# FFN up as seven products of half-size blocks, its convolution summed in PSUM, and FFN down with its first two tiles together in the second half too

## The reference

```
x = x + g1 * out_x                        # end of the mixer
hx = modulate(rms_norm(x, norm2_g), sh2, sc2)
gate, val = split(hx @ ffn_w_up, 2)       # ffn_w_up: 1024 x (2 * 2816)
gate = dwconv_grid(gate, w, b, 16, 64)    # 3x3 taps per channel on a 16 x 64 grid of tokens
x = x + g2 * ((silu(gate) * val) @ ffn_w_down)
return rms_norm(x, final_g)               # goes into the attention layer
```

## Time and profile before

| | us |
|---|---|
| median of 3 runs | 2507.32 |
| profiled execution, whole | 2507.99 |
| its span, first to last instruction | 2506.2 |
| PE busy in the span | 2241.5 (89%) |
| DVE busy | 1478.6 (59%) |
| ACT busy | 853.1 (34%) |
| POOL busy | 568.2 (23%) |

### The profile page before, as it was taken

How to read it: one execution, slowest core, us unless ns; L and a number is a source line. 1 busy time by engine, 2 the same in 40 slices (tenths; PEclk the granted TensorE clock), 3 DMA queues, 4 the chain that set the end, 5 groups by cost and what they waited for, 6 DMA issues and landing times. The chain is left out here.

```text
span 2506.2 us, 44088 instructions
## 1 busy us (share of the span) xinstructions
PE 2241.5 (89%) x18248; PEld 1768.3 (71%) x18248; DVE 1478.6 (59%) x1876; ACT 853.1 (34%) x1290; POOL 568.2 (23%) x275
## 2 busy tenths in 40 slices
PE   6879999658999998899999978978999999999898
PEld 1657677558889766778878766856777676676566
DVE  5877766787666346666666652055364755645644
ACT  3343444223232345233323322144333443423321
POOL 0333443200003042222222212423332111011111
PEclk9889999879999999999999988989999999999999
DMA  6543325466665410122122224343222111111512
GB/s 262 211 156 138 123 97 165 149 155 165 148 169 118 151 62 17 51 75 73 52 75 75 75 82 161 95 143 115 70 93 76 34 51 51 38 48 43 185 68 76
DMA packets 246567, 262.76 MB, mean 105 GB/s; under 512 B 156920, under 2 KB 188280, under 8 KB 242048
## 3 DMA queue, kind: packets, MB, share of 16 engines
q1 hardware_dynamic: 241792, 243.55, 30.3%
q10 hardware_dynamic: 4608, 16.78, 1.9%
HBM read 196.29 MB, written 64.00 MB: 104 GB/s over the span
## 5 line engine op out<-in xcount | busy, mean ns | idle before, releaser
L105 PE MATMUL b_ps<-h_hi,b_wpool 128*128 128x512 f32 (+1 forms) x976 | 301.4, 386 | 18.5 <-issue 7.5
L2034 DVE SCALAR_TENSOR_TENSOR e_acc<-e_grid,vec,e_acc 128x1024 f32<-128x1024 f32 x176 | 265.5, 1509 | 42.8 <-DVE e_acc L2034 37.4
L2557 PE MATMUL g_ps<-g_h_hi,w 128*128 128x512 f32 x784 | 262.3, 406 | 4.9 <-ACT g_q L2750 4.9
L105 PEld LDWEIGHTS b_ps<-h_hi,b_wpool 128*128 128x128 f32 x976 | 182.7, 192 | 67.4 <-issue 20.4
L105 PE MATMUL e_gates<-h,e_w_hi 128*128 128x512 f32 x672 | 210.0, 394 | 14.7 <-POOL e_w_lo L1873 14.5
L105 PE MATMUL e_vars<-h,e_w_hi 128*128 128x512 f32 x672 | 206.9, 389 | 0.0
L1873 POOL TENSOR_TENSOR e_w_lo<-e_raw_up,e_w_hi 128x1024 fp32r<-128x1024 f32 x44 | 115.6, 2627 | 377.4 <-ACT e_w_hi L1809 377.4
L2870 POOL TENSOR_TENSOR w<-raw_down,w 128x1024 fp32r<-128x1024 f32 x38 | 94.3, 2483 | 462.9 <-ACT w L2728 462.9
L105 PE MATMUL b_ps<-h_lo,b_wpool 128*128 128x512 f32 (+1 forms) x488 | 184.8, 379 | 0.0
L2111 PE MATMUL g_pb<-g_z_hi,g_down_hi 128*128 128x512 f32 x330 | 136.9, 415 | 48.2 <-POOL g_down_lo L2253 29.5
L2557 PEld LDWEIGHTS g_ps<-g_h_hi,w 128*128 128x128 f32 x784 | 150.0, 191 | 41.2 <-ACT g_q L2750 5.6
(11 more groups left out here) (360 smaller groups left out, 4796.8 us busy)
## 6 DMA issues: line engine op xcount, KB each, us to landing
e_raw_up<-w_ffn SPq DMA_DIRECT2D x22, 1024.0 KB, 5.1
raw_down<-w_down SPq DMA_DIRECT2D x32, 704.0 KB, 4.1
c_op<-ops SPq DMA_DIRECT2D x40, 512.0 KB, 4.3
raw_down<-w SPq DMA_DIRECT2D x38, 512.0 KB, 3.3
b_xin<-ada_rows ACTq DMA_DIRECT2D x32, 512.0 KB, 5.2
ops<-b_xin SPq DMA_DIRECT2D x16, 1024.0 KB, 4.1
raw_in<-w SPq DMA_DIRECT2D x26, 512.0 KB, 4.2
zs<-e_z SPq DMA_DIRECT2D x22, 512.0 KB, 2.6
```

The source lines that it names most:

```text
L105: last = nc.tensor.matmul(out, w[:, k, :], x[:, k, cols], start=(k == 0 and n == 0), stop=(k == nk - 1 and n == 2))
L2034: a = STT(out=acc[:], in0=view, scalar=wt, in1=acc[:], op0=ALU.mult, op1=ALU.add)
L2557: mm = nc.tensor.matmul(out_bank, ww[w % 2][:, k], xx[g][:, k], start=(k == 0 and a == 0), stop=(k == KD - 1 and a == 2))
```

## The change

**Seven products.** For tiles 1 to 21 the product of a tile is taken as a 2x2 block product. A is the weight tile: rows gate and val, columns the two halves of the 8 k-tiles. B is the normalised input: the two halves of k, and the two token halves. With S1 = A21+A22, S2 = S1-A11, S3 = A11-A21, S4 = A12-S2 and T1 = B12-B11, T2 = B22-T1, T3 = B22-B12, T4 = B21-T2 the products are P1 = A11 B11, P5 = S1 T1, P6 = S2 T2, P7 = S3 T3, P2 = A12 B21, P3 = S4 B22, P4 = A22 T4, in this order on PE, each 4 k-tiles times 3 passes = 12 matmuls. The outputs are C11 = P1+P2, u2 = P1+P6, u4 = u2+P5, C12 = u4+P3, u3 = u2+P7, C21 = u3+P4, C22 = u4+P7. Tile 0 is computed as before. Six PSUM banks take the products in turn.
- Per tile POOL gets 4 sums (`sum_w`) and 7 remainders (`up_low`), of 512 columns each, in place of 2 of 1024. ACT gets 7 splits of 512 columns (`up_high`), a copy of P1, and the first tap. `raw` is one buffer still; its next load waits for POOL's last remainder of the tile.
- T1 to T4 are made once, by DVE, split by ACT (`t_high`) and POOL or DVE (`t_low`), 2048 columns each. Their high parts lie in `w_2`, so x is stored in `x1s` before (two stores of 2 MB) and loaded again in FFN down.
- The loops are written out; `hold` and the register-valued waits go.

**Convolution in PSUM.** `acc` lies in the two banks of `vars_`. ACT writes the first tap there; DVE's other eight read and write it there. DVE makes the seven sums (u2, u4, u3, C22, C11, C12, C21), each of one SBUF tensor and one bank, between the taps; C11 and C12 go into `grid`, the val blocks into SBUF, so the last multiplication has two SBUF inputs.

**Norm.** `whole` has a buffer for each token half; `normed_high` has two ACT instructions for every k; `sums(1)` moves from behind the second product of tile 0 into the middle of its first.

**FFN down.** Units 16 to 19 (tiles 0 and 1 of half 1) run interleaved like units 0 to 3, with a third bank for tile 1; `square_sums(0)` stands behind them. Loads and splits of weights move forward among the z loads: units 4 and 5, and 16 to 19. x is loaded per half (2 MB each), half 0 behind the first two z loads.

```diff
+            def product_of(i, n):
+                slot, (x_hi, x_lo) = PRODUCTS[n]
+                pe.wait_ge(sem(f"w_lo{slot}"), made(slot, i))
+                bank_free(i, n)
...
+                for k in range(CONV):
+                    for m, (w, x) in enumerate(((w_hi, x_hi), (w_hi, x_lo), (w_lo, x_hi))):
+                        mm = nc.tensor.matmul(bank_of(i, n), w[slot][:, k], x[:, k], start=(k == 0 and m == 0), stop=(k == CONV - 1 and m == 2))
+                mm.then_inc(sem("prod"), 1)
...
+            def load_up(i):
+                sp.wait_ge(sem(f"w_lo{A22}"), i)
+                sp.dma_start(raw[:], d["w_ffn"][i]).then_inc(sem("raw"), 16)
...
@@ ACT @@
+            for i in range(1, NFF):
+                first_kept(i)
+                for slot in (A11, S1, S2) if i + 1 < NFF else ():
+                    up_high(slot, i + 1)
+                silu(i - 1)
+                for slot in (S3, A12) if i + 1 < NFF else ():
+                    up_high(slot, i + 1)
+                first_tap(i)
+                for slot in (S4, A22) if i + 1 < NFF else ():
+                    up_high(slot, i + 1)
+            silu(NFF - 1)
...
@@ POOL @@
+            for i in range(2, NFF):
+                sum_w(S1, i)
+                sum_w(S2, i)
+                up_low(A11, i)
+                sum_w(S3, i)
+                up_low(S1, i)
+                sum_w(S4, i)
+                for slot in (S2, S3, A12, S4, A22):
+                    up_low(slot, i)
...
@@ DVE @@
+            t_sum(T1)
+            t_sum(T3)
+            t_sum(T2)
+            t_low(T1)
+            t_sum(T4)
+            t_low(T3)
+            for i in range(1, NFF):
+                taps(i - 1, range(1, 2))
+                if i > 1:
+                    c21(i - 1)
+                taps(i - 1, range(2, 6))
+                sum_u2(i)
+                taps(i - 1, range(6, 7))
+                sum_u4(i)
+                taps(i - 1, range(7, 8))
+                sum_u3(i)
+                taps(i - 1, range(8, 9))
+                c22(i)
+                c11(i)
+                c12(i)
+                gated_up(i - 1)
+            taps(NFF - 1, range(1, 2))
+            c21(NFF - 1)
+            taps(NFF - 1, range(2, 9))
+            gated_up(NFF - 1)
...
-    UNITS = G0 + [(1, j, b) for j in range(KD) for b in range(2)]
+    UNITS = G0 + [(1, j, b) for _, j, b in G0]
...
+        for g in range(HALVES):
+            for b in range(2):
                 for j in range(2):
+                    unit_there(pe, NG * g + 2 * b + j)
+                for k in range(PART):
                     z_there(pe, g, PART * b + k)
+                    for j in range(2):
+                        unit(pe, NG * g + 2 * b + j, k)
+            if g:
                 square_sums(pe, 0)
```

More of the change, by code:

```diff
@@ L1543, in mix_up @@
         part_ps = [st.enter_context(nc.psum_tensor(f"e_part{n}", [P, BANK], F32)) for n in G]
[L1544 to L1547, removed]
+        first_ps = [v[:, cols(g)] for v in (vars_, gates) for g in G]
+        banks = [part_ps[0][:], part_ps[1][:]] + [means[:, cols(g)] for g in G] + first_ps[2:4]
@@ L1690, in _ @@
                 scan_part(1, n)
[L1691 to L1696, removed]
+            for n, (s, g) in enumerate(UP_FIRST):
+                for slot in ((A11, A12), (S1, A22))[s]:
+                    pe.wait_ge(sem(f"w_lo{slot}"), 1)
                 for k in range(KD):
@@ L1800, in _, with up_high @@
                 w2_high(n)
-            def split_hi(n, s):
-                if isinstance(n, int):
+            def up_high(slot, i):
+                if i == 0:
                     act.wait_ge(sem("raw_first"), 16)
-                else:
[L1807 to L1823, removed]
+                elif slot in (A11, A12, A22):
+                    act.wait_ge(sem("raw"), 16 * i)
+                else:
+                    act.wait_ge(sem("sum_w"), 4 * (i - 1) + (S1, S2, S3, S4).index(slot) + 1)
+                if i == 1 and slot in (S3, S4):
+                    act.wait_ge(sem("pre"), 2 * KD)
+                if i == 1 and slot in FIRST:
+                    act.wait_ge(sem("prod"), {A11: 3, A12: 3, S1: 4, A22: 4}[slot])
+                elif i > 1:
+                    act.wait_ge(sem("prod"), base(i - 1) + made_by[slot])
+                A(w_hi[slot], a_of[slot] if i == 0 else source[slot], ACT.Copy).then_inc(sem(f"w_hi{slot}"), 1)
@@ L1953, in normed_low, with all_low @@
[L1953 to L1954 removed]
+                dve.wait_ge(sem("n_hi"), KD * g + k + 1)
+                TT(lo[:, k, cols(g)], whole[g][:, k], hi[:, k, cols(g)].bitcast(F32), ALU.subtract).then_inc(sem("n_lo0"), 1)
+            def all_low(g):
+                for par in range(2):
+                    dve.wait_ge(sem(f"n_lo{par}"), CONV * (g + 1))
@@ new lines, in t_low, with taps @@
+            def t_low(n):
+                dve.wait_ge(sem(f"t_hi{n}"), 1)
+                if n == T1:
+                    dve.wait_ge(sem(f"t_whole{T2}"), 1)
+                TT(t_lo[n], t_whole[n], t_hi[n].bitcast(F32), ALU.subtract).then_inc(sem(f"t_lo{n}"), 1)
+            w_conv = t["v_ffn_conv_w"]
+            def taps(i, part):
+                for tap in part:
+                    dy, dx = tap // 3, tap % 3
+                    view = grid[:, dy:dy + GRID_H, dx:dx + GRID_W]
+                    wt = w_conv[:, i + tap * NFF:i + tap * NFF + 1]
+                    if tap > 1:
+                        dve.wait_ge(sem("conv"), 8 * i + tap - 1)
+                    else:
+                        dve.wait_ge(sem("first_tap"), i + 1)
+                    STT(out=acc, in0=view, scalar=wt, in1=acc, op0=ALU.mult, op1=ALU.add).then_inc(sem("conv"), 1)
```

407 lines of the change are left out of this document (280 added, 127 removed).

## The result

| | before | after |
|---|---|---|
| median of the runs, us | 2508.44 (4 runs, 2506.58 to 2513.89) | 2448.88 (4 runs, 2447.09 to 2454.7) |
| profiled execution, us | 2507.99 | 2447.09 |
| its span, us | 2506.2 | 2445.2 |
| mean granted clock of the span | 0.951 | 0.954 |

The ratio is 0.9763, with a 95% interval of 0.974 to 0.9786: faster by 2.4%. Split at the points at which the forecast split it, the spans differ so (us). The forecast put P1 of tile 2 of the kernel before at 1041.3, and the table keeps that point; in the trace that tile's first matmul starts at 1041.6, which would make the two differences beside it +0.8 and -52.3.

The account below looks back on a forecast made before the run. POOL's eleven instructions plus weight load, 20.6 us per tile against PE's 19.04, were taken as the new bound. Loop -36.8, start +2.9, end +11.5, FFN down +3 total -19.4: from 2507.99 to 2488.6, forecast 2488, range 2461 to 2510.

Parts of the forecast that it names:

- the POOL ring: FFN up loop: POOL's eleven instructions and the weight load in series, 20.6 us per tile; bounds 19.04 (PE) and 22.0.
- the exposed load: FFN up loop: SP's issue 0.25, load 5.2 and start 0.1 us, in series with POOL's instructions in each tile.
- the price of FFN down: FFN down: +2 us in half 0, +1 in half 1, together +3; bounds -7 and +27.
- the start of the last taps: End of FFN up: the last convolution's taps begin 3 us after the last matmul.
- The loop: FFN up, P1 of tile 2 to last matmul: 410.4 us against 447.2, so -36.8.
- Rival A: FFN up loop: PE is the bound after all, 27 us less, 2461 us; chance 0.15.
- Rival C: FFN up loop: taps on PSUM are slower; at 0.5 us more per tap, 2520 us; chance 0.05.
- PE's idle 1.5 us per tile: FFN up loop: PE waits 1.5 us before P1 of each tile for POOL; wrong if PE waits within a tile.
- The start: Tiles 0 and 1 of FFN up: tile 2 starts at 1044.2, +2.9 us; bounds -6 and +12, the latter with slow clock.
- The end: Last matmul of FFN up to last z: 17.1 us where it was 5.6, so +11.5 (10 to 14).
- The stall before `square_sums(0)`: FFN down, half 1: PE waits 15 us for the squares; unit 20 starts at 1698.5, as before; stall moved, +1.
- Rival B: FFN down: z phases get longer and the kernel slower, 2512 us at the bound of 27; chance 0.10.

Follow-up runs that it names:

- the three experiments above: Each on the changed kernel: next weights loaded one POOL instruction earlier, 2442.39 us; one more POOL subtraction per tile, 2477.7 us; 4 of 84 matmuls left out, 2452.18 us.
- mix_order2: Changed kernel with the mixer's order of the kernel before in full, on DVE and ACT: 2452.06 us.
- combined_all: Changed kernel with earlier weight load, reordered tile 1, `square_sums(0)` after two units, last tile's P7 after P2 and P3, T2 and T4 remainders on DVE: 2416.26 us.
- taps_sbuf: Changed kernel with the convolution's running sum back in its own SBUF buffer: 2552.52 us.
- pool_twice: Changed kernel with one more POOL subtraction of 512 columns per tile from tile 2 on: 2477.7 us.

## Why the prediction was wrong, step by step

The direction and most mechanisms were right, the POOL ring as the new bound above all; four sizes were off, all to the same side, and one edit was not priced at all. The steps that failed are the exposed load in the ring's sum, the price of FFN down, the start of the last taps, and the mixer, which was put at nothing. Forecast and measured spans differ by 41.7 us: 15.8 in the loop, 9.7 in FFN down, 5.1 in the mixer, 4.8 in the rest, 4.5 at the end and 1.8 at the start.

**The loop (forecast -36.8, measured -52.6).** The ring was the right bound (the three experiments above), but of 19.72 us and not of 20.6. The term that was mis-sized is the load: "SP's issue 0.25, load 5.2, start 0.1", 5.55, where POOL idles 4.9. All three parts are shorter in the changed kernel. In the kernel before SP issued the load 0.24 us after POOL's last remainder ended (median of 19 tiles; in rows 4 and 6, 1185.94 and 1186.18), and it landed 5.04 us later in the median, 5.19 in the mean; so 0.25 and 5.2 were read rightly from a loop that is rolled up. In the changed kernel the issue comes 0.03 us after the remainder, which ends at 1205.62:

```profile
1205.65 0.33 SPq L1624 DMA_DIRECT2D e_raw_up<-w_ffn  x1
```

The load lands 4.81 us later in the median, and POOL's sum starts 0.07 behind that: 4.91. The 0.24 went together with the rolled loop, like the gap between dependent taps; that the one caused the other, and why the load itself is 0.2 to 0.4 shorter, no run isolates. The remaining 0.3 is the multiplications, which hold POOL off for 0.45 each and not for 0.6. 0.88 us over 19 tiles is 16.7, less 0.9 for the last tile, which took 19.9 and not 19.0: the whole difference. Rival A (PE is the bound) had 19.04 for PE; it is 19.27, 0.229 per matmul and not 0.227. The reading of rows 3 was right for the kernel before, whose tiles without a wait took 21.76, 0.227 for each of 96; in the changed kernel some products run at 0.230 to 0.235 per matmul, and why stays open. The 2461 of this rival was made up of that one change, with all other terms as forecast.

**POOL and DVE.** POOL busy 14 us of a tile, idle only behind the load, taps unstretched on PSUM, multiplications stretched: all as said. Rival C (taps on PSUM cost more) is out: 160 taps in the loop lie between 1276 and 1292 ns. What I had not seen is how much hangs on it; with the sum in SBUF the change would have lost 44 us (2552.52 against 2508.44). PE's idle 1.5 us per tile was too long, and it was put at the wrong place: it is 0.45 (19.72 less 19.27), in pieces of some 0.1 around the first matmuls of P5 and P6, and of P1 in some tiles. So PE does wait within a tile, which the prediction names as a sign that it is wrong.

By the Trainium skill, "VectorE: DVE Perf Modes", section "The TRN2 errata", a VectorE instruction from PSUM to SBUF has a fixed cost of 120 cycles, and one from SBUF to SBUF of 58. The taps that read and write PSUM at 1285 ns (median) against 1285 on SBUF do not agree with that, nor do the sums, which go from PSUM to SBUF in 0.68 us, as the folds of FFN down do with all operands in SBUF.

**The start (+2.9, measured +1.1).** Order and reasons were right: P1 of tile 1 34.3 us behind tile 0's first matmul (forecast 35.6), P5 45.7 (47.6), tile 2 65.0 (66.8). Tile 0 itself took 28.3 and not 26.1. The slow clock, which stood in the upper bound alone, came: 0.77 over tile 1, with matmuls 0.43 apart behind both stalls.

**The mixer (0, measured -5.1).** The step that failed is one that I left out: the diff moves `normed(3)` and `with_bonus(3)` on DVE and `mix_high(1)` on ACT. The section on the change does not list this, and I priced none of it. The rows to see it were in the trace of before: a wait of 5.78 us on DVE in front of two instructions that do not need it. mix_order2 gives all of it back (5.8 for 5.7); 0.6 of it is hidden in the table because the first centring began 0.6 later (859.4, before 858.8).

**The end (+11.5, measured +7.0).** "Its taps begin 3 us after the last matmul" was wrong: they begin 0.7 before its end. I took the time from the ring, where silu stands behind the splits of a tile to come. The last tile has none: silu ran at 1427.9, the multiplication 1.9 later and unstretched, and the first tap beside it. The chain itself took 13.4 (forecast 14.1).

**FFN down (+3, measured -6.7).** The stall before `square_sums(0)` is there, 16.4 us for a forecast of 15. What failed is the price of the two things around it. Half 0: I took 5.5 for x's 2 MB and 4 for the weights ahead, +2 in all; the reload costs 2.7 until unit 4, which starts 53.6 us after the last z and not 56.0, so -2.4. Half 1: I had the squares end as late as now and the three more POOL remainders cost something, +1 in all; it is -4.3. In both kernels two pairs of folds are stretched to 3.0 by remainders, so these cost nothing more, and the folds end 4.0 us earlier, counted from FFN down's first matmul, 2.9 of it won by the start of unit 4. PE, which now waits for them, starts unit 20 2.9 us behind the last fold, where it was 5.7 before. Rival B, by which these phases get longer, is out.

**The rest (0, measured -4.8).** This is not the change. In the profiles of the changed kernel and of the twelve experiments, whose code is the same from there on, this stretch took 700.6 to 711.6 us, and the 707.3 of before lies among them. Nothing was tried to find out what moves it. So some 5 us of the distance between these two profiles is chance.

With the sum of independent terms each uncertain by 5 to 15 us, and the low end taken from one rival alone, the range was too narrow: the low end should have held the ring at its own lower bound of 19.04 (29.6 us) together with FFN down at its -7 (10 us), which gives 2448.

## What to carry to other kernels

When an engine is bound to a load by a single buffer, add up the ring instruction by instruction, and the load in three parts: from the last instruction's end to the issue, from there to landing, and from landing to the first use (0.03, 4.8 and 0.07 us here). When the change alters how the loop is written, the first part, read from the rolled loop (0.24), may not hold. Go through the diff for every instruction that changes places, also outside the part that the change is about; an instruction that waits in front of others that need nothing of it is worth its wait (5.7 us here, and 15 in FFN down). And where DVE and POOL both have work on SBUF they take turns, so moving work from one to the other bought 2 us in its stretch and nothing that the run times show (`combined_all`), while the sum in PSUM is worth 104.

## What the runs showed of the hardware

- DVE with a PSUM sum in and out runs beside POOL without loss (1.29 us per tap of 1024 columns). With all operands in SBUF a tap takes 2.2 and POOL's instruction of 512 columns 2.27, and both start every 2.23 us where POOL's alone start every 1.25 us. A DVE instruction of 2.28 beside POOL's of 1.25 makes 3.3 for both.
- PE's pauses of 2.2 to 4.4 us in each tile of `taps_sbuf` went with a granted clock of 0.93 over the loop; those of 1.2 to 1.6 in 19 of 20 tiles of `pool_twice` left it at 1.00.
- In the rolled loop SP's issue came 0.24 us after the instruction it waited for, and a dependent tap 0.24 after the one before; with the loop written out it is 0.03 and none.
- A matmul of three in turn (two activations, two weights, 128x512) takes 0.229 us over a tile of the changed kernel at the full clock, and 0.227 over a tile of the kernel before.
